# Delta rule: where and how the 16x16 diagonal blocks are inverted

## The reference, cut to what matters

```python
L = jnp.where(strict, jnp.einsum('bhnid,bhnjd->bhnij', kb, k) * decay, 0.0)
A = L + jnp.eye(C)
tri = lambda rhs: lax.linalg.triangular_solve(A, rhs, left_side=True, lower=True, unit_diagonal=True)
u = tri(vb)
w = tri(kb * jnp.exp(gc)[..., None])
...
# scan over chunks, once per direction:
v_new = u_i - w_i @ state
o = (q_i * exp(gc_i)) @ state + attn_i @ v_new
state = state * exp(g_last) + k_dec.T @ v_new
```

## Time and profile before

| what | value |
| --- | --- |
| median of 3 runs | 1139.9 us (1139.21 to 1139.95) |
| profiled execution | 1140.08 us, its span 1138.0 us |
| PE matmul busy | 1068.7 us, 94% |
| DVE busy | 556.9 us, 49% |
| ACT busy | 378.6 us, 33% |
| POOL busy | 104.9 us, 9%, 139 instructions |
| mean granted TensorE clock | 0.972 |
| chain that ended last | PE 84%, DVE 10%, issue 2%, ACT 2%, DMA 1%, POOL 1% |
| VectorE product of 512 elements (`gate_act` by PSUM, L1856, x22) | mean 0.696 us |
| latent attention | about 228 to 332 us |
| scan, groups 0 to 3 | about 332 to 473 us |

### The profile page before, as it was taken

The page is one execution under the profiler, slowest core; times in us unless marked ns, Lnnn a source line. Parts: engine busy times, 40 slices in busy tenths (PEclk is TensorE's granted clock), DMA queues, the critical chain, the costliest instruction groups (busy, mean ns, idle before and its releaser), DMA issues.

```text
span 1138.0 us, 14290 instructions
## 1 busy us (share of the span) xinstructions
PE 1068.7 (94%) x5878; PEld 898.7 (79%) x5878; DVE 556.9 (49%) x805; ACT 378.6 (33%) x563; POOL 104.9 (9%) x139
## 2 busy tenths in 40 slices
PE   8899999999885988899999999989999999999995
PEld 6789798767674878787888888878888888888884
DVE  5884446466768767845425253453333333232314
ACT  5545544744331221244222232252223222221212
POOL 4000001424222223100000000000000000000000
PEclk9999999999898999899999999989999999999998
DMA  9323320000000001311423233523332333332301
GB/s 294 105 63 95 111 66 2 1 2 10 5 16 1 11 1 38 112 56 37 130 74 111 83 103 111 185 74 92 94 111 75 111 101 84 111 111 74 111 19 74
DMA packets 103999, 87.17 MB, mean 77 GB/s; under 512 B 13109, under 2 KB 93697, under 8 KB 103936
## 3 DMA queue, kind: packets, MB, share of 16 engines
q1 hardware_dynamic: 102288, 81.80, 23.7%
q0 software_dynamic: 1488, 4.40, 1.1%
q10 hardware_dynamic: 160, 0.07, 0.0%
HBM read 83.64 MB, written 2.62 MB: 76 GB/s over the span
## 4 chain that ended last, share of the span: by engine, by line
PE 84%; DVE 10%; issue 2%; ACT 2%; DMA 1%; POOL 1%; SPq 0%; DVEq 0%; ACTq 0%
PE psum L869 22%; PE psum L870 22%; PE psum L871 22%; PE psum L997 3%; PE psum L1015 2%; PE psum L1005 2%; PE psum L1196 2%; PE psum L1223 1%; DVE block_p L1856 1%; PE psum L1279 1%; PE psum L1267 1%; PE psum L1148 1%; DVE Zx L1856 1%; DVE Xm L1856 1%; PE psum L1068 1%
## 5 line engine op out<-in xcount | busy, mean ns | idle before, releaser
L869 PE MATMUL psum<-hT_hi,w_hi 128*128 128x512 f32 (+1 forms) x712 | 279.9, 393 | 7.6 <-DVE w_lo L1856 5.9
L1856 DVE TENSOR_TENSOR w_lo<-w_raw,w_hi 128x2048 fp32r<-128x2048 f32 (+2 forms) x81 | 167.4, 2067 | 231.1 <-ACT w_hi L1434 231.1
L870 PE MATMUL psum<-hT_lo,w_hi 128*128 128x512 f32 (+1 forms) x712 | 278.7, 391 | 0.0
L871 PE MATMUL psum<-hT_hi,w_lo 128*128 128x512 f32 (+1 forms) x712 | 278.6, 391 | 0.0
L1434 ACT ACTIVATE w_hi<-w_raw 128x2048 fp32r<-128x2048 f32 (+2 forms) x82 | 141.3, 1724 | 163.5 <-PE psum L871 151.7
L869 PEld LDWEIGHTS psum<-hT_hi,w_hi 128*128 128x128 f32 (+1 forms) x712 | 134.2, 188 | 38.0 <-DVE w_lo L1856 7.2
L871 PEld LDWEIGHTS psum<-hT_hi,w_lo 128*128 128x128 f32 (+1 forms) x712 | 134.2, 188 | 28.7
L870 PEld LDWEIGHTS psum<-hT_lo,w_hi 128*128 128x128 f32 (+1 forms) x712 | 134.2, 188 | 28.0
L1856 DVE TENSOR_TENSOR psum<-gate_act,psum 128x512 f32<-128x512 f32 x22 | 15.3, 696 | 120.4 <-PE psum L871 120.4
L869 PE MATMUL psum<-w_hi,act_hi 128*128 128x512 f32 x176 | 68.5, 389 | 0.0
L870 PE MATMUL psum<-w_lo,act_hi 128*128 128x512 f32 x176 | 68.5, 389 | 0.0
(11 more groups left out here) (300 smaller groups left out, 1647.7 us busy)
## 6 DMA issues: line engine op xcount, KB each, us to landing
w_raw<-in_w_in_dram SPq DMA_DIRECT2D x23, 1024.0 KB
w_raw<-in_ffn_w_gate_up_dram SPq DMA_DIRECT2D x44, 512.0 KB
w_raw<-in_ffn_w_down_dram SPq DMA_DIRECT2D x10, 1024.0 KB
w_raw<-in_mem_w_kv_dram SPq DMA_DIRECT2D x4, 1024.0 KB
w_raw<-in_w_out_dram SPq DMA_DIRECT2D x4, 1024.0 KB
x_tok<-in_x_dram SPq DMA_DIRECT2D x4, 512.0 KB, 5.5
w_raw<-in_w_branch_mla_dram SPq DMA_DIRECT2D x4, 512.0 KB
w_raw<-in_w_branch_dn_dram SPq DMA_DIRECT2D x4, 512.0 KB
```

The lines of the kernel that those rows point to most:

```text
L869: pe.matmul(o, s_hi, m_hi, start=first, stop=False)
L870: pe.matmul(o, s_hi, m_lo, start=False, stop=False)
L871: return pe.matmul(o, s_lo, m_hi, start=False, stop=last)
L1856: return dve.tensor_tensor(o, a, b, op)
```

## The change

VectorE's block work (ones on the diagonal, doubling, joining) is taken out of the attention loop and of the scan, and `block_p` and one semaphore with it. GpSimd does all of it in another way. `split_blocks` masks both triangles as before; then for k = 1 to 14 `eliminate(k)` takes column k above the diagonal (k entries) times the rest of row k (15 - k entries), for both directions in one instruction, and adds the result to the corner: a multiplication and an addition of 2·k·(15 - k) elements in each partition. `join_blocks` sets the diagonal to one and adds the two directions. Each of these instructions waits for the one before (`link`), except the last. In GpSimd's order, half 0 is split and eliminated for k = 1 to 7 behind `join(2, .)`, and for k = 8 to 14 and joined behind `triangles(3, .)`; `split_blocks(0)` stood ahead of `join(2, .)`. Half 1 is done whole behind `first_chosen(0, .)`, ahead of `scan_inputs(0)` and the scan's first triangles. GpSimd's two waits for `inverse_ready` go.

```diff
@@ -760,15 +757,28 @@
                 lt = LT[g][:, p, :, :]
                 pool.tensor_tensor(lt, lt, dec_lo[:, p, :, :], ALU.add).then_inc(lt_ready, 1)
 
+            blocks = block_fb[:, :, 0:BLOCK * BLOCK].rearrange("p d (i k) -> p d i k", i=BLOCK)
+            whole = block_in[:, :].rearrange("p (i k) -> p i k", i=BLOCK)
+
             def split_blocks(q):
                 pool.wait_ge(blocks_in[q], 16)
-                if q > 0:
-                    pool.wait_ge(inverse_ready, q)
-                square_of = lambda a: a.rearrange("p (i k) -> p i k", i=BLOCK)
-                whole = square_of(block_in[:, :])
                 for d, src in ((0, whole), (1, whole.rearrange("p i k -> p k i"))):
-                    pool.affine_select(out=square_of(block_fb[:, d, 0:256]), in_=src, compare_op=ALU.is_ge, fill=0.0, base=-1,
-                                       pattern=[[-1, BLOCK], [1, BLOCK]], channel_multiplier=0).then_inc(block_masked, 1)
+                    ins = pool.affine_select(out=blocks[:, d], in_=src, compare_op=ALU.is_ge, fill=0.0, base=-1,
+                                             pattern=[[-1, BLOCK], [1, BLOCK]], channel_multiplier=0)
+                    link(ins)
+
+            def eliminate(k):
+                n = BLOCK - 1 - k
+                column = blocks[:, :, 0:k, k:k + 1].broadcast_to([P, 2, k, n])
+                row = blocks[:, :, k:k + 1, k + 1:BLOCK].broadcast_to([P, 2, k, n])
+                term = block_t[:, 0:2 * k * n].rearrange("p (d i j) -> p d i j", d=2, i=k)
+                corner = blocks[:, :, 0:k, k + 1:BLOCK]
+                link(pool.tensor_tensor(term, column, row, ALU.mult))
+                link(pool.tensor_tensor(corner, corner, term, ALU.add))
+
+            def join_blocks():
+                link(pool.memset(block_fb[:, 0, :].rearrange("p (i s) -> p i s", s=BLOCK + 1)[:, 0:BLOCK, 0:1], 1.0))
+                pool.tensor_tensor(whole, blocks[:, 0], blocks[:, 1].rearrange("p i k -> p k i"), ALU.add).then_inc(inverse_ready, 1)
 
             def by_block(n):
                 return masks[:, n, :].rearrange("p (k c) -> p k c", c=BLOCK).unsqueeze(1).broadcast_to([P, 4, P // BLOCK, BLOCK])
@@ -804,7 +814,6 @@
                 for d in range(2):
                     t = tile_of(g, d)
                     if 0 < g < NT - 1:
-                        pool.wait_ge(inverse_ready, 2)
                         released(pool, ("KV", g - 1, d))
                         sv, gv = (b[:, d, :, :].rearrange("p j (u n) -> p (j u) n", u=2) for b in (state, state_g))
                         pool.tensor_tensor(gv, sv, heads(egl[:, col(t, d):col(t, d) + 8]), ALU.mult).then_inc(sg_ready, 1)
@@ -817,12 +826,18 @@
                     if g > 0:
                         pool.wait_ge(lt_ready, 2 * g - 1 + p)
                     triangles(g, p)
+                if g == NT - 1:
+                    for k in range(8, BLOCK - 1):
+                        eliminate(k)
+                    join_blocks()
                 if g + 1 < NT:
                     scale_keys(g + 1)
+                for p in range(2):
+                    join(g, p)
                 if g == 2:
                     split_blocks(0)
-                for p in range(2):
-                    join(g, p)
+                    for k in range(1, 8):
+                        eliminate(k)
             for t in range(NT):
                 released(pool, ("tok", t, 2))
             pool.memset(state[:, :, :, :], 0.0).then_inc(state_zero, 1)
@@ -831,6 +846,9 @@
             for p in range(2):
                 first_chosen(0, p)
             split_blocks(1)
+            for k in range(1, BLOCK - 1):
+                eliminate(k)
+            join_blocks()
             filled(pool, ("mla", "S", NT * H - 1))
             scan_inputs(0)
             for g in range(NT):
@@ -2152,67 +2170,6 @@
...
-            def block_parts(b):
-            def block_terms(q, b, left, right):
-            def block_right_terms(q, b):
-            def block_right_sums(q, b):
-            def block_left_terms(q, b):
-            def block_left_sums(q, b):
-            def block_right(q, b):
-            def block_left(q, b):
...
-            def block_ones(q):
-                dve.wait_ge(block_masked, 2 * q + 2)
-                link(dve.memset(diag[:, :, 0:1], 1.0))
-
-            def block_joined(q):
-                link(dve.memset(diag[:, BLOCK:2 * BLOCK, 0:1], 0.0))
-                square_of = lambda a: a.rearrange("p (i k) -> p i k", i=BLOCK)
-                tt(square_of(block_in[:, :]), square_of(block_fb[:, 0, 0:256]),
-                   square_of(block_fb[:, 1, 0:256]).rearrange("p i k -> p k i"), ALU.add).then_inc(inverse_ready, 1)
-
             def beside_attention(n):
                 m = n - 1
                 if n == -1:
@@ -2229,25 +2186,6 @@
                             upper(g, p)
                         elif i == 4:
                             lower(g, p)
-                if n == INVERT0:
-                    block_ones(0)
-                    block_right(0, 2)
...
-                elif n == INVERT0 + 9:
-                    block_left_sums(0, 8)
-                elif n == INVERT0 + 10:
-                    block_joined(0)
 
             attention("mla", H, NT, NT * (MH - 1), beside_attention)
 
@@ -2376,28 +2314,12 @@
                         gap("A", g, 1)
                         if last > 0:
                             scan_queries(last)
-                    if g == 0 and s == 4:
-                        block_ones(1)
-                        block_right(1, 2)
-                        block_left(1, 2)
-                    if g == 0 and s == 5:
-                        block_right(1, 4)
-                        block_left(1, 4)
-                    if g == 0 and s == 6:
-                        block_right_terms(1, 8)
-                    if g == 1 and s == 4:
-                        block_left_terms(1, 8)
-                    if g == 1 and s == 5:
-                        block_left_sums(1, 8)
-                        block_joined(1)
                     if g == NT - 1 and s == 6:
                         prep(("z", 0))
                 inverse_done(g)
                 if last >= 0:
                     scan_update(last)
                 scores(g, 1)
-                if g == 0:
-                    block_right_sums(1, 8)
             scan_keys(NT - 1)
             scan_queries(NT - 1)
             prep(("z", 1))
```

More of the change, by code:

```diff
@@ L47 @@
 VALUES0 = PREP0 + 5 * NT
-INVERT0 = 16
 TWO_PI = 2 * np.pi
@@ L418, in hybrid_encoder_kernel @@
         kb_tok = in_ring("kb_tok", [P, 2, 512], 40)
-        block_p = [in_ring("block_p0", [P, 1024], 44), v("block_p1", [P, 1024], 20)]
         block_n = nc.dram_tensor("block_n", (NT, H, P // BLOCK, BLOCK, BLOCK), F32, kind="Internal").ap()
@@ L496, in hybrid_encoder_kernel @@
         blocks_in = [sem(f"blocks_in{q}") for q in range(2)]
-        block_masked = sem("block_masked")
         inverse_ready = sem("inverse_ready")
@@ L2153, in lower @@
                 tt(dec_lo[:, p, :, :], dec_lo[:, p, :, :], quad(key), ALU.mult).then_inc(free(key), 1)
-            flat = block_fb[:, :, :].rearrange("p d s -> p (d s)")
-            diag = flat.rearrange("p (i s) -> p i s", s=BLOCK + 1)
-            def block_parts(b):
-                corner = flat.rearrange("p (m s) -> p m s", s=34 * b)[:, :, 0:32 * b].rearrange("p m (i w) -> p m i w", w=BLOCK)
-                return corner[:, :, 0:b, 0:b], corner[:, :, 0:b, b:2 * b], corner[:, :, b:2 * b, b:2 * b]
@@ L2177, in block_right_terms @@
-            def block_right_terms(q, b):
-                x11, n12, x22 = block_parts(b)
-                block_terms(q, b, n12, x22)
-            def block_right_sums(q, b):
-                link(dve.tensor_reduce(block_t[:, 0:16 * b], block_p[q][:, 0:16 * b * b].rearrange("p (a j) -> p a j", j=b), AX.X, ALU.add))
-            def block_left_terms(q, b):
-                x11, n12, x22 = block_parts(b)
-                order = "p (m i k) -> p m i k" if b == 8 else "p (i m k) -> p m i k"
-                block_terms(q, b, x11, block_t[:, 0:16 * b].rearrange(order, m=16 // b, i=b))
@@ L2198, in block_right @@
-            def block_right(q, b):
-                block_right_terms(q, b)
-                block_right_sums(q, b)
-            def block_left(q, b):
-                block_left_terms(q, b)
-                block_left_sums(q, b)
-            def block_ones(q):
-                dve.wait_ge(block_masked, 2 * q + 2)
-                link(dve.memset(diag[:, :, 0:1], 1.0))
-            def block_joined(q):
-                link(dve.memset(diag[:, BLOCK:2 * BLOCK, 0:1], 0.0))
-                square_of = lambda a: a.rearrange("p (i k) -> p i k", i=BLOCK)
-                tt(square_of(block_in[:, :]), square_of(block_fb[:, 0, 0:256]),
-                   square_of(block_fb[:, 1, 0:256]).rearrange("p i k -> p k i"), ALU.add).then_inc(inverse_ready, 1)
```

## The result

The changed kernel takes 1118.4 us (median of 4 runs, 1115.9 to 1119.7) against 1139.6 for the kernel before; the ratio is 0.9819, 95% interval 0.9801 to 0.9837. The forecast was 1119.5 us. The profiled execution took 1119.67 us, its span is 1117.9 us, 20.1 less than before.

A forecast was written before the change was run, and what follows sets the result against it. PE was taken to bound most of the span, with VectorE's block work on the path in places. Attention 9.7 plus scan group 0 10.8 gave 20.5 us off 1140.08: forecast 1119.5 us, range 1115.5 to 1126.5.

The forecast's parts named there:

- Attention, 9.7 us: Attention loop: with half 0's block work off VectorE, it ends 9.7 us earlier, at 322.7 instead of 332.4.
- The two parts: Attention's two stretches: 6.2 us from the five iterations with block work (23.4 to 17.2), 3.5 from those behind (27.2 to 23.6).
- Rival D: Attention: PE's clock falls all the same, so its 4.5 us stay and the kernel takes 1124 us; chance 0.09.
- Scan's group 0, 10.8 us: Scan group 0: 11.3 us of VectorE block work goes, less 0.5, so it takes about 23.5 us instead of 34.2.
- The wait of `scores(0, 0)` for GpSimd: Scan group 0, behind `T1`: VectorE waits 0.3 us for GpSimd's triangles of p = 1.
- Counting nothing in group 1: Scan group 1: block work of 2.5 and 1.9 us counted as no gain, covered by PE's recurrence products.
- GpSimd's price, 12.4 us a half: GpSimd's elimination of each half: 11.7 us from fitted rows and links plus 0.7 for short rows; bounds 9.7 to 37.5.
- Cover of 14.9 us: GpSimd holds no path while an elimination takes under about 14.9 us; every us beyond costs two.
- The slack of `upper(3, .)`: End of attention: GpSimd's `triangles(3, .)` finishes 0.5 to 1.1 us before VectorE reaches `upper(3, .)`, at about 296.6.
- Rival B: GpSimd bounds attention's end and group 0: 1125.7 us at an 18 us elimination, 1139.7 at 25; chance 0.14.
- C: Attention's end and group 0: elimination above 25.2 us leaves no gain, 1145.7 us at 28; chance 0.04.
- Timetable: From half 0's blocks to the scan: `block_x` at 309.7, `Zs` at 313.8, attention's end at 322.7 us.

The follow-up runs named there:

- e4: Changed kernel plus two small VectorE products (32 elements, result unused) at attention iteration 16, beside GpSimd's join: 1123.1 us, ratio 0.9864.
- e8: Changed kernel plus two small unused VectorE products at iteration 10, where GpSimd idles: 1117.8 us, ratio 0.9826.
- e6: Changed kernel plus two extra GpSimd products behind k = 6 and behind k = 9 in each half: 1117.8 us, ratio 0.9829.
- e3: Against the kernel before: column-by-column elimination for both halves, but on VectorE where the doubling stood: 1131.0 us, ratio 0.9931.
- e1: Changed kernel with half 0 inverted on VectorE by doubling again, half 1 still on GpSimd: 1125.7 us, ratio 0.9886.
- e5: Changed kernel plus two more GpSimd products behind every k in both halves: 1135.6 us, ratio 0.9992.
- e9: Changed kernel plus 10 idle 128x128 PE products ahead of the first product of scan groups 1, 2 and 3: 1112.4 us, ratio 0.9784.
- the last two kernels: The two follow-up kernels measured last; beside them the kernel before had a median of 1136.08 us (15 runs).

## Why the prediction was right

**Attention, 9.7 us:** 9.8 measured. The two parts were put at 6.2 and 3.5 and measured 5.9 and 3.9; that the errors of 0.3 and 0.4 us cancel is luck. That the wait for `dec` would go and the clock stay up came true (e4 and e8 show the chain from the stretched products to the lower clock). Rival D, that the clock falls all the same, is out for the two traced executions of this kernel.

**Scan's group 0, 10.8 us:** 11.0 measured. The wait of `scores(0, 0)` for GpSimd, put at 0.3, was 0.26. Counting nothing in group 1 was right (33.1 and 33.2 us), and nothing came from the clock there: the shorter wait, 2.67 us instead of 6.72, still brought it down.

**GpSimd's price, 12.4 us a half:** 11.7 measured, which is the fit without the surcharge I had put on short rows. The line through 64 and 512 elements, 0.235 us for 28 and 0.415 for 112, met 0.24 and 0.41. What I left open, the patterns with four dimensions and rows of one element, cost nothing that these rows show. Only the joining, 256 elements with one input read in transposed order, took 0.85 us where the line gives 0.72.

**Cover of 14.9 us:** 13.6 cost nothing, 23.4 cost 17.8 to 18.6 us where the rule says 17.0. The margin was a little too wide; 14.2 fits both runs. The slack of `upper(3, .)`, put at 0.5 to 1.1 us, was 2.1: its first instruction needs only the first pair of triangles, done at 295.28, and stands at 297.33. By the prediction's own numbers an elimination of 14.9 us (1.2 us more ahead of those triangles) would already have made it wait, so that text was not consistent there; e6, with `triangles(3, .)` 1 us later, shows no such wait. Rival B's and C's mechanism exists, with its places (`upper(3, .)` and, on the chain, `scores(0, 0)`) and its price; the elimination is only too short for it. That GpSimd is twice as slow would have been the wrong price: at 52 and 72 elements the ratio is 1.3 to 1.4 (e3), and the elimination is less work.

**Timetable:** `block_x` predicted at 309.7, was 309.50; `Zs` 313.8 and 314.06; attention's end 322.7 and 323.2. Part of this closeness is luck: this trace runs 0.5 us late from the start, GpSimd was 0.7 us a half quicker than priced, and from `block_x` to `Zs` it took 4.56 us instead of 3.95.

## What to carry to other kernels

Read the cost of work on a busy engine from what the stage loses, not from its busy time: 12.7 us of VectorE work in the attention cost 9.8 us (about 4 of them through PE's clock: 5.9 in the first part, less the wait of 1.91), 11.3 in group 0 cost 11.0, the rest in group 1 nothing. Before work goes to an idle engine, write its whole timetable with what is queued behind it and find how much slower it may be before it holds up something; here that margin (14.9 against 12.4) is what the forecast stood on. And where PE waits for 2.7 to 3 us each round and its clock falls, a counted handful of idle products in the gap can keep the clock up: 10 ahead of each of three groups gained about 5 us, as they ended before the real work could begin.

## What the runs showed of the hardware

- A small VectorE instruction with two SBUF inputs that starts beside a GpSimd addition of 512 elements lasts until about the end of that addition: 2.0 to 2.2 us for two of 32 elements beside two such additions (before, e4), 0.28 to 0.41 apart from them. In e3 the first ended at 283.17 and the second at 284.39, GpSimd's two additions at about 283.1 and 284.35. VectorE's instructions with one input in PSUM kept 0.68 us beside GpSimd.
- PE's clock fell to its lower level (1.2 GHz) behind waits of 1.6 to 3.5 us in most cases, but not in all: not behind 2.15 and 2.81 us (e3), 2.95 (e1), 2.98 (e5) and 3.45 (e9). What decides was not settled.
- The scatter of several us among runs of one kernel goes with the mean granted clock. Of the 15 runs of the kernel before beside the last two kernels, the four of 1133.0 to 1135.2 us show 0.976 to 0.978, the four of 1138.4 to 1140.6 us 0.969 or 0.970. At which waits the clock differs was not traced.
- A 128x128 product of f32 by f32 shows as two rows of the trace, 0.22 us together at the upper clock (22 of them take 5.08 us and 10 take 2.40). A transpose of the same size takes 0.11 us (8 of them 1.04 us and 4 of them 0.61).
